# Attention scores from split float32r operands on the whole array, with new places for gates and probabilities

## What is computed

```python
def block(qi):
    ...
    s_c = jnp.einsum('bghqd,bgcd->bghqc', qb, k_cmp) * scale + bias_gh[:, :, rel_bucket(dist_c)]
    p_c = masked_softmax(s_c, dist_c >= 0, -1)
    ...
    s_s = jnp.einsum('bghqd,bgqnkd->bghqnk', qb, k_g) * scale + bias_s
    p_s = masked_softmax(s_s, (dist_s >= 0)[:, :, None], (-2, -1))
    o_s = jnp.einsum('bghqnk,bgqnkd->bghqd', p_s, v_g)
    ...
    s_w = jnp.einsum('bghqd,bgkd->bghqk', qb, kw) * scale + bias_gh[:, :, rel_bucket(dist_w)]
    p_w = masked_softmax(s_w, valid_w, -1)
    o_w = jnp.einsum('bghqk,bgkd->bghqd', p_w, vw)
    return gb[..., 0:1] * o_c + gb[..., 1:2] * o_s + gb[..., 2:3] * o_w
```

## Time and profile before

| | us |
|---|---|
| median of three executions | 803.28 |
| the profiled execution, its own time | 803.57 |
| its span, first to last instruction | 801.8 |
| TensorE busy | 794.7 (99%) |
| POOL busy | 489.2 (61%) |
| VectorE busy | 398.9 (50%) |
| ScalarE busy | 198.2 (25%) |

### The profile page before, as it was taken

The page is one execution under the profiler, slowest core; times in us unless marked ns, Lnnn a source line. Parts: engine busy times, 40 slices in busy tenths (PEclk is TensorE's granted clock), DMA queues, the critical chain, the costliest instruction groups (busy, mean ns, idle before and its releaser), DMA issues.

```text
span 801.8 us, 12380 instructions
## 1 busy us (share of the span) xinstructions
PE 794.7 (99%) x4644; PEld 632.9 (79%) x4644; DVE 398.9 (50%) x565; ACT 198.2 (25%) x405; POOL 489.2 (61%) x325
## 2 busy tenths in 40 slices
PE   8999999999999999999999999999999999999998
PEld 6788877988787666578888888888888888888886
DVE  5794588834465445634457576671000476650000
ACT  6101753314311445725022222210000122210000
POOL 5666544676454755556666576676666676666663
PEclk9999999999999999999999999999999999999999
DMA  8244222233422010015323323223323223323320
GB/s 281 96 138 159 81 82 80 79 106 111 178 81 78 27 53 28 1 54 184 105 80 105 105 80 105 94 90 105 95 88 105 91 93 105 103 80 132 131 78 26
DMA packets 23549, 78.01 MB, mean 97 GB/s; under 512 B 2723, under 2 KB 3499, under 8 KB 23380
## 3 DMA queue, kind: packets, MB, share of 16 engines
q1 hardware_dynamic: 19964, 69.00, 25.9%
q10 hardware_dynamic: 3544, 8.44, 2.9%
HBM read 75.31 MB, written 4.21 MB: 99 GB/s over the span
## 4 chain that ended last, share of the span: by engine, by line
PE 97%; DVE 1%; POOL 1%; DMA 1%; issue 0%; SPq 0%; ACT 0%; DVEq 0%; POOLq 0%
PE bank L387 27%; PE bank L389 26%; PE bank L388 26%; PE bank L721 3%; PE bank L743 3%; PE bank L764 2%; PE bank L481 1%; PE bank L482 1%; PE bank L483 1%; PE bank L530 1%; DMA x<-in_xT 1%; POOL wsp L307 1%; PE bank L411 1%; PE bank L637 1%; PE bank L753 1%; PE bank L696 1%
## 5 line engine op out<-in xcount | busy, mean ns | idle before, releaser
L307 POOL TENSOR_TENSOR wsp<-wraw,wsp 128x1024 fp32r<-128x1024 f32 x124 | 305.7, 2466 | 10.4
L305 POOL TENSOR_SCALAR wsp<-wraw 128x1024 fp32r<-128x1024 f32 x124 | 135.3, 1091 | 241.2 <-PE bank L389 156.5
L387 PE MATMUL bank<-hhi,wsp 128*128 128x512 f32 x352 | 140.9, 400 | 1.6 <-DVE hlo L1163 0.8
L388 PE MATMUL bank<-hlo,wsp 128*128 128x512 f32 x352 | 137.5, 391 | 0.0
L389 PE MATMUL bank<-hhi,wsp 128*128 128x512 f32 x352 | 137.3, 390 | 0.0
L387 PE MATMUL bank<-ghi,wsp 128*128 128x512 f32 x256 | 100.3, 392 | 0.0
L388 PE MATMUL bank<-glo,wsp 128*128 128x512 f32 x256 | 99.7, 389 | 0.0
L389 PE MATMUL bank<-ghi,wsp 128*128 128x512 f32 x256 | 99.7, 389 | 0.0
L387 PE MATMUL bank<-uhi,wsp 128*128 128x512 f32 x256 | 99.7, 389 | 0.0
L388 PE MATMUL bank<-ulo,wsp 128*128 128x512 f32 x256 | 99.6, 389 | 0.0
L389 PE MATMUL bank<-uhi,wsp 128*128 128x512 f32 x256 | 99.6, 389 | 0.0
(11 more groups left out here) (249 smaller groups left out, 1009.6 us busy)
## 6 DMA issues: line engine op xcount, KB each, us to landing
wraw<-in_w SPq DMA_DIRECT2D x126, 512.0 KB, 3.3
bias_skewed<-bias_lines ACTq DMA_DIRECT2D x1, 2048.0 KB
bias<-bias_skewed ACTq DMA_DIRECT2D x1, 2048.0 KB, 8.9
x<-in_xT ACTq DMA_DIRECT2D x1, 2048.0 KB, 8.1
out<-x ACTq DMA_DIRECT2D x8, 256.0 KB, 2.0
x<-in_xT SPq DMA_DIRECT2D x3, 512.0 KB, 6.8
x<-in_xT SPq DMA_DIRECT2D x2, 256.0 KB, 4.3
wraw<-in_w SPq DMA_DIRECT2D x4, 128.0 KB, 7.5
```

The costliest lines, as they stand in the source:

```text
L305: pool.tensor_scalar(whi[:, two, :], wraw[:, raw, :], 1.0, 0.0, ALU.mult, ALU.add).then_inc(w_hi, 1)
L307: pool.tensor_tensor(wlo[:, two, :], wraw[:, raw, :], whi[:, two, :].bitcast(F32), ALU.subtract).then_inc(w_split, 1)
L387: pe.matmul(out_, wh, mh, start=first, stop=False)
L388: pe.matmul(out_, wh, ml, start=False, stop=False)
```

## The change

`scores(t)` becomes two float32r matmuls per group on all 128 rows of the array. The stationary operand `q_stack[g]` holds, for group g, the high part of the queries in the group's own 64 rows and the low part in the other 64. The moving operand of the first matmul is the high part of the keys, standing in both halves, that of the second the low part in both halves. So the two sums hold all four products of high and low parts. The parts are made during the compression: ACT copies a normed tensor into bank 6 or 7 and its rounded parts into SBUF (`part_high`: three instructions for queries, five for keys), DVE subtracts (`part_low`: two instructions), and for keys ACT copies the low part into the other half later (`key_low_again`: two). That is done for q0 to q3, ks and kw: 26 instructions on ACT and 12 on DVE.

Bank 6 takes the output sums of squares, which leave the list `users`. The b gates get an array of their own, the probabilities, the output's parts and `o_ring` other places in SBUF, and the transposed probabilities one buffer each (`pt_low`, `pt_high`) where there were two. The gate of a projection of the table is evacuated one turn later, behind that turn's shifts.

```diff
-        PAIR_BANKS = {"st_ks": 2, "st_kw": 3, "st_q0": 4, "st_q1": 5}
+        OWN_BANK = {"st_ks": 2, "st_kw": 3, "st_q0": 4, "st_q1": 5, "st_o0": 6, "st_o1": 6, "st_o2": 6, "st_o3": 6}
...
+            def output_stat(h):
+                pe.wait_ge(part_lo, PART["kw"] + 1)
+                pe.wait_ge(pair_read, 4 + h)
+                stat(f"st_o{h}", ones[:], sq[:, h % 2, :], to=bank[6])
...
+                if t == 0:
+                    pe.wait_ge(part_lo, len(PARTS))
+                    pe.wait_ge(k_ready, 4)
                 for g in range(2):
-                    rows = slice(64 * g, 64 * g + 64)
                     if t >= 2:
                         pe.wait_ge(s_shift[g], t - 1)
-                    pe.matmul(score_bank(t, g)[:, 0:n], qn[rows, i, qb * P:qb * P + P], keys[b][rows, 0:n],
-                              start=True, stop=True).then_inc(s_done[g], 1)
+                    for part in range(2):
+                        last = pe.matmul(score_bank(t, g)[:, 0:n], q_stack[g][:, i, qb * P:qb * P + P],
+                                         k_parts[b][part][:, g, 0:n], start=part == 0, stop=part == 1)
+                    last.then_inc(s_done[g], 1)
...
+            def part_high(name):
+                n = PART[name]
+                source, tiles = part_source(name), part_tiles(name, 0)
+                act.wait_ge(normed, {"ks": 1, "kw": 2}[name] if name[0] == "k" else 3 + int(name[1]))
+                if n < 2:
+                    act.wait_ge(sc_kept[n], 8)
+                else:
+                    act.wait_ge(part_lo, n - 1)
+                act.activation(part_bank(name)[:], source, ACT.Copy)
+                for g in range(2 if name[0] == "k" else 0):
+                    own, other = slice(64 * g, 64 * g + 64), slice(64 - 64 * g, 128 - 64 * g)
+                    act.activation(tiles[g][other, :], source[own, :], ACT.Copy)
+                for g in range(2):
+                    own = slice(64 * g, 64 * g + 64)
+                    last = act.activation(tiles[g][own, :], source[own, :], ACT.Copy)
+                last.then_inc(part_hi, 1)
...
             for h in range(HG):
                 copy_256(h)
+            part_high("q0")
+            part_high("q1")
             copy_hidden(0)
+            part_high("ks")
+            part_high("q2")
             gelu_exp(0)
...
+            part_high("kw")
+            part_high("q3")
             copy_hidden(1)
             inverse_rms("st_kc", DH, 64)
...
                 if h < 2:
                     square_o(h + 2)
+                    key_low_again(("ks", "kw")[h])
...
-                if gi >= 2:
-                    act.wait_ge(pv_done[0], 2 * (gi - 2) + qb // 2 + 1)
-                to = (pt_low, pt_high)[qb // 2][gi % 2]
+                if gi >= 1:
+                    act.wait_ge(pv_done[0], 2 * (gi - 1) + qb // 2 + 1)
+                to = (pt_low, pt_high)[qb // 2]
...
+            def part_low(name):
+                dve.wait_ge(part_hi, PART[name] + 1)
+                for g in range(2):
+                    own, other = slice(64 * g, 64 * g + 64), slice(64 - 64 * g, 128 - 64 * g)
+                    to = part_tiles(name, 1)[g][own if name[0] == "k" else other, :]
+                    last = dve.tensor_tensor(to, part_bank(name)[own, :],
+                                             part_tiles(name, 0)[g][own, :].bitcast(F32), ALU.subtract)
+                last.then_inc(part_lo, 1)
+
             gate_g(0)
+            part_low("q0")
+            part_low("q1")
             gate_g(1)
             gelu(0)
             gate_g(2)
+            part_low("ks")
+            part_low("q2")
+            part_low("kw")
+            part_low("q3")
             gate_g(3)
...
-                if t in GB_AFTER:
-                    if t < NT:
-                        invert(t)
-                    if GB_AFTER[t] != "gb7":
-                        gate(GB_AFTER[t])
+                if t in GB_AFTER and t < NT:
+                    invert(t)
+                if t - 1 in GB_AFTER and GB_AFTER[t - 1] != "gb7":
+                    gate(GB_AFTER[t - 1])
```

More of the change, by code:

```diff
@@ L232, in build_block @@
         gel_ready, cmp_out, kcn_ready, vc_ready = (sem(n) for n in ("gel_ready", "cmp_out", "kcn_ready", "vc_ready"))
+        part_hi, part_lo, k_ready = sem("part_hi"), sem("part_lo"), sem("k_ready")
         cs_done, cs_shift, cp_ready, cp_scaled, cpT_done, cpT_copied = (
@@ L249, in build_block @@
         users = ["f2", "q2", "f3", "q3"]
-        users = users + ["kc", "vc", "ks", "kw", "nq0", "nq1", "nq2", "nq3", "st_q2", "st_q3", "g0", "g1", "g2", "cmp_k", "g3", "st_kc", "ga0", "st_o0", "cmp_v"]
-        for h in range(1, HG):
-            users += [f"ga{h}", f"st_o{h}"]
+        users = users + ["kc", "vc", "ks", "kw", "nq0", "nq1", "nq2", "nq3", "st_q2", "st_q3", "g0", "g1", "g2", "cmp_k", "g3", "st_kc", "ga0", "cmp_v", "ga1", "ga2",
+                          "ga3"]
         users += ["ga4", "ga5", "ga6", "ga7", "gb0", "gb1"]
@@ L261, in build_block @@
         U0 = len(users)
-        PAIR_BANKS = {"st_ks": 2, "st_kw": 3, "st_q0": 4, "st_q1": 5}
+        OWN_BANK = {"st_ks": 2, "st_kw": 3, "st_q0": 4, "st_q1": 5, "st_o0": 6, "st_o1": 6, "st_o2": 6, "st_o3": 6}
         def bank_of(name):
-            return bank[PAIR_BANKS[name] if name in PAIR_BANKS else USE[name] % 2]
+            return bank[OWN_BANK[name] if name in OWN_BANK else USE[name] % 2]
         def score_bank(t, g):
@@ L271, in p_tile, with part_source, part_tiles, part_bank @@
         def p_tile(t, g, n):
-            return p_ring[:, t % 4, g, 0:n] if t % 4 < 3 else p_last[g][:, 0:n]
+            return p_ring[t % 4][:, g, 0:n] if t % 4 < 3 else p_last[g][:, 0:n]
+        PARTS = ["q0", "q1", "ks", "q2", "kw", "q3"]
+        PART = {name: n for n, name in enumerate(PARTS)}
+        def part_source(name):
+            return {"ks": ksn[:], "kw": kwn[:]}[name] if name[0] == "k" else qn[:, int(name[1]), :]
+        def part_tiles(name, low):
+            if name[0] == "k":
+                parts = k_parts["sw".index(name[1])][low]
+                return [parts[:, g, :] for g in range(2)]
+            return [q_stack[g][:, int(name[1]), :] for g in range(2)]
+        def part_bank(name):
+            return bank[6 + PART[name] % 2]
         block = ctx.enter_context(nc.Block())
@@ L416, in stat_pair @@
                 stats[0] += 2
-                to = [bank_of(name) if name in PAIR_BANKS else claim(name) for name in (a, b)]
+                to = [bank_of(name) if name in OWN_BANK else claim(name) for name in (a, b)]
                 for n in range(2):
@@ L665, in _ @@
             project("ga0")
-            stat("st_o0", ones[:], sq[:, 0, :])
+            output_stat(0)
             pe.wait_ge(csum, 2)
@@ L677, in _ @@
                 project(f"ga{h}")
-                stat(f"st_o{h}", ones[:], sq[:, h % 2, :])
+                output_stat(h)
             def q_tile(h, qb):
@@ L757, in values @@
                 i, b = divmod(gi, 2)
-                pt = (pt_low, pt_high)[half][gi % 2]
+                pt = (pt_low, pt_high)[half]
                 for g in range(2):
@@ L1019, in copy_256, with key_low_again @@
                                ACT.Copy).then_inc(sc_kept[h % 2], 1)
+            def part_high(name):
[14 more added lines that the diff above has]
+                last.then_inc(part_hi, 1)
+            def key_low_again(name):
+                act.wait_ge(part_lo, PART[name] + 1)
+                for g, tile in enumerate(part_tiles(name, 1)):
+                    own, other = slice(64 * g, 64 * g + 64), slice(64 - 64 * g, 128 - 64 * g)
+                    act.activation(tile[other, :], tile[own, :].bitcast(F32), ACT.Copy).then_inc(k_ready, 1)
             for h in range(HG):
                 copy_256(h)
+            part_high("q0")
+            part_high("q1")
             copy_hidden(0)
+            part_high("ks")
+            part_high("q2")
             gelu_exp(0)
@@ L1101, in _ @@
             for n in range(4):
-                g_ = gates[:, n % 2, 4 * (n // 2):4 * (n // 2) + 4, :]
+                g_ = gates[n % 2][:, 4 * (n // 2):4 * (n // 2) + 4, :]
                 act.activation(g_, g_, ACT.Sigmoid).then_inc(gate_sig, 1)
@@ L1375, in gate @@
             def gate(name):
-                scaled(name, gates[:, "ab".index(name[1]), int(name[2]), :])
+                scaled(name, gates["ab".index(name[1])][:, int(name[2]), :])
             gate("ga0")
@@ L1396, in _ @@
                 o_ = o_ring[:, h % 2, :]
+                if h == 0:
+                    dve.wait_ge(o_done, HG)
                 if h >= 2:
```

36 lines of the change are left out of this document (20 added, 16 removed).

## The result

| | before | after |
|---|---|---|
| median of six executions each, us | 803.50 | 797.42 |
| lowest to highest, us | 803.26 to 804.33 | 797.18 to 797.66 |
| the profiled execution / its span, us | 803.57 / 801.8 | 797.66 / 795.9 |

The ratio is 0.9923, 95% interval 0.9913 to 0.9933: 6.1 us less, where 5.5 were forecast (797.8).

The account below looks back on a forecast made before the run. TensorE's start-to-start distances bound the kernel: scores 4.9 + bank 0.7 + gates 0.3 - lost again 0.4 = 5.5 us off a median of 803.3, so 797.8 us; own range 796.6 to 799.5, overall range 796.6 to 802.0.

Parts of the forecast that it names:

- The bound: Whole kernel: time is the sum of TensorE's start-to-start distances; what moves no start of a matmul costs nothing.
- Scores: Attention loop, 32 steps: four float32r matmuls per step and fewer changes of array shape save 4.9 us together.
- lost again: Head pair branches: evacuations ending just as transposes want the bank cost 0.05 us in each of 8, 0.4 (0 to 1.5).
- Steps 1 to 3: Start of the attention loop: 0.55 us saved of a possible 0.9, since a shift hangs on DVE.
- change-of-shape term: Scores behind transposes: staying whole array to whole array saves 0.14 us per such place.
- Own bank: Output sums in bank 6: projections no longer wait for DVE's evacuation at three places, 0.7 us saved.
- Gates: Attention loop: gates evacuated later on DVE give back 0 to 0.3 us; 0.3 taken.
- Work in the compression: 26 copies on ACT and 12 subtractions on DVE fit in idle time and waits: price 0.
- (a): Rival, scores of 128 columns: float32r needs as many passes as plain, 3.4 us more, 801.2 us; chance 0.26.
- (b): Rival, attention loop: DVE, ACT and POOL pace it, half of 4.9 us or more returns as waits, 800.7 us; chance 0.12.
- (c): Rival, compression: eight ACT copies before the second hraw delay fold_hidden(1), slower at 804.9 us; chance 0.04.
- (d): Rival, scores: float32r between plain float32 costs 0.15 us at each of 32 steps, 4.8 us go, 802.6 us; chance 0.04.

Follow-up runs that it names:

- e_scores: The changed kernel with the old scores, one plain float32 matmul per group on 64 rows, and no parts made: 802.36 us, ratio 0.9985.
- e_one: The changed kernel with one score matmul per group, the low part of the keys left out (output not the reference's): 792.71 us, ratio 0.9864.
- e_halves: The changed kernel with scores as three float32r matmuls per group on its 64 rows, low by low left out, fewer copies: 800.51 us, ratio 0.9961.
- e_gates: The changed kernel with each b gate evacuated in its own turn, directly behind its projection, as before: 799.02 us, ratio 0.9942.
- e_act8: The changed kernel with eight more ACT copies in front of the copies of kw and q3: 802.75 us, ratio 0.999.
- e_gate8: The changed kernel with eight more ACT copies before those of kw and q3, and gate g3 before their subtractions on DVE: 801.44 us, ratio 0.9969.
- e_act4: The changed kernel with four more ACT copies in front of the copies of kw and q3: 798.46 us, ratio 0.9938.
- e_fill8: The changed kernel with eight more ACT copies before those of kw and q3, and mixed_values(2) done twice to occupy TensorE: 801.48 us, ratio 0.9971.

## Why the prediction was right

**The bound** held: the gain is a sum of start-to-start distances on TensorE.

**Scores**: 4.9 with 0.4 lost again, so 4.5 forecast, and 4.8 measured (e_scores against after). Place by place from the timelines of turns 16 to 19: 512 columns behind transposes 0.28 (forecast 0.29), 256 behind transposes 0.23 (0.30; 0.25 at the other six places), 384 behind values 0.03 (0.05), 128 behind values -0.08 (-0.15). The signs and the order are right. The 256 was priced a little high: there the next transposes wait for ACT's copy, as the rows beside e_one show. Steps 1 to 3 gave some 0.4 for 0.55. Against that stand the 128, priced too dear, and the two transposes behind the scores of 512 columns, 0.03 cheaper at seven places, which I hadn't priced. So the sum is nearer than its terms, and in that there is some luck. What carries it is the change-of-shape term, 0.14 at each of 13 places; e_halves, which changes the shape again, took 800.5 us although its scores are cheaper.

**Own bank**: mis-sized, 0.7 forecast and 0.9 measured. I compared the first matmuls behind the sums; with its bank free the projection also starts inside the sum's overlap, which the other row shown, st_o0 with values behind it, couldn't tell.

**Gates**: 0.3 forecast; worth 0.4 in the old loop (e_scores) and 1.6 in the new one (e_gates). I costed the deferral in the old loop, and the scores in a loop that already had it. The total comes out by that, but the two don't simply add: the deferral covers what the shorter turns would expose. Without the deferral the new scores would have brought 109.80 - 106.18 = 3.6 us of the 4.9, so 1.3 lost again, near the upper bound of 1.5 that I gave that term.

**Work in the compression**: priced at 0, and so it was. The cover on ACT was 1.27 us, 1.5 forecast; copies took 0.60 and pairs 1.27. But I named only `hraw` as a deadline. The gate g3, which I took as no concern until ga0 begins, is the nearer of the two: it ends at 187.66, 1.8 us before ga0, whereas `hraw` had 1.27 us and another 1.85 to the fold.

**Rivals**: (a) is refuted by the rows at 314.61: 0.11 us at 128 columns, not 0.22. (b) did not happen at its price, but its mechanism is there: in after the steps of 256 columns are set by ACT's copy, e_one shows more of it next door, and e_gates shows it with the old place of the gates. (c) didn't happen; its price was too low, since past the cover an idle TensorE also loses its clock. (d) is refuted: with 0.15 us lost at each step the 4.8 us of the scores couldn't be there.

## What to carry over

Where small matmuls stand between whole-array work, read the rows in front of and behind them as well as their own: here, in turns 16 to 19, the scores' own distances moved between -6% and +19% with the width, and the gain was in the transposes before them. When an engine's share of a turn gets shorter, price every evacuation in the other engines' queues again in the new turn, since an order that cost 0.4 us in the old loop cost 1.6 in the new one. And when work goes in front of something in a queue, look at everything that stands behind it there: the nearest deadline here was DVE's gate, not the copy on ACT.

## What the runs showed of the chip

- A float32r matmul of 128 moving columns follows another after 0.11 us, as fast as one of 256 columns (0.12); at 512 it is 0.23.
- float32r matmuls on the two row halves run beside each other: six of 512 columns in 0.89 us, where six whole ones at 0.23 would be 1.4.
- Eight whole-array transposes take 1.02 us in front of row halves (before, e_halves) and 0.80 in front of whole-array float32r matmuls (after); four take 0.59 and 0.38.
- A wait of 2.1 us (e_act8) and of 2.2 us (e_gate8) brought TensorE's clock to the 1.2 GHz level in the profiled executions, until 6.7 and 4.2 us after the wait, and cost 2.3 and 1.6 us more than the wait. In three of e_gate8's nine executions the mean granted clock was 1.000. Waits of 0.9 us (e_act4) and 1.2 us (e_fill8) left it at 2.4 GHz.
